# A hybrid HGRN2 and differential attention block: score copies ahead of the q and k update, a forget-gate half one slot later, two remainders three slots later

## The reference

```python
mod = jax.nn.silu(c) @ w_ada[l] + b_ada[l]
shift, scale, gate = jnp.split(mod, 3, axis=-1)
h = rms_norm(x, g_pre[l]) * (1.0 + scale[:, None, :]) + shift[:, None, :]
proj = h @ w_in[l]                       # 1024 x 6144
hq, hf, hi, hg, dq, dk, dv, dg, ma, mb = jnp.split(proj, split_idx, axis=-1)
...
o_a = hgrn2_chunked(hq, k_in, hi, log_f)     # S_t = diag(f_t) S_{t-1} + k_t v_t^T, o_t = S_t^T q_t, 4 heads of 128
o_b = diff_attention(dq, dk, dv, lam)        # (softmax(q1 k1) - lam softmax(q2 k2)) v, causal, 4 heads
...
y = jax.nn.sigmoid(ma) * (o_a @ w_branch_a[l]) + jax.nn.sigmoid(mb) * (o_b @ w_branch_b[l])
x = x + gate[:, None, :] * rms_norm(y @ w_out[l], g_post[l])
```

## Time and profile before

| what | us |
|---|---|
| three runs | 887.14, 888.22, 893.91 (median 888.22) |
| the profiled execution | 888.69 |
| its span, first to last instruction | 886.8 |
| busy: PE, DVE, POOL, ACT | 843.5, 608.5, 478.4, 471.7 |

### The profile page before, as it was taken

How to read it: one execution, slowest core, us unless ns; L and a number is a source line. 1 busy time by engine, 2 the same in 40 slices (tenths; PEclk the granted TensorE clock), 3 DMA queues, 4 the chain that set the end, 5 groups by cost and what they waited for, 6 DMA issues and landing times. The chain is left out here.

```text
span 886.8 us, 13086 instructions
## 1 busy us (share of the span) xinstructions
PE 843.5 (95%) x4781; PEld 664.3 (75%) x4781; DVE 608.5 (69%) x712; ACT 471.7 (53%) x861; POOL 478.4 (54%) x363
## 2 busy tenths in 40 slices
PE   2899889999999999999999999999999999999997
PEld 2687678777777777777777777777788888887885
DVE  3888984788794888694897866864500166697775
ACT  7676323786443875445865336745455641333453
POOL 6054685455464455554545653566787822236884
PEclk9899899999999999999999999999999999999999
DMA  9914131102101101110120121021211561302222
GB/s 327 342 45 147 50 94 48 49 1 72 49 15 58 48 14 59 49 48 24 48 72 1 49 72 32 17 72 49 71 48 48 180 224 47 95 24 95 96 95 95
DMA packets 75586, 68.11 MB, mean 77 GB/s; under 512 B 3652, under 2 KB 65156, under 8 KB 75524
## 3 DMA queue, kind: packets, MB, share of 16 engines
q1 hardware_dynamic: 75408, 67.25, 23.6%
q10 hardware_dynamic: 116, 0.03, 0.0%
HBM read 58.88 MB, written 8.39 MB: 76 GB/s over the span
## 5 line engine op out<-in xcount | busy, mean ns | idle before, releaser
L624 POOL TENSOR_TENSOR w_lo<-w_raw,w_hi 128x512 fp32r<-128x512 f32 x140 | 193.5, 1384 | 258.7 <-ACT w_hi L1197 257.2
L935 PE MATMUL pj<-b_hi,w_hi 128*128 128x512 f32 x712 | 299.7, 421 | 6.3 <-DVE dk L1599 3.4
L937 PE MATMUL pj<-b_hi,w_lo 128*128 128x512 f32 x712 | 279.6, 393 | 0.0
L936 PE MATMUL pj<-b_lo,w_hi 128*128 128x512 f32 x712 | 279.0, 392 | 0.0
L935 PEld LDWEIGHTS pj<-b_hi,w_hi 128*128 128x128 f32 x712 | 134.4, 189 | 49.3 <-issue 12.5
L937 PEld LDWEIGHTS pj<-b_hi,w_lo 128*128 128x128 f32 x712 | 134.2, 188 | 30.0
L936 PEld LDWEIGHTS pj<-b_lo,w_hi 128*128 128x128 f32 x712 | 134.8, 189 | 25.6 <-issue 3.1
L1197 ACT ACTIVATE w_hi<-w_raw 128x512 fp32r<-128x512 f32 x132 | 82.8, 627 | 63.5 <-PE pj L937 57.4
L605 POOL TENSOR_TENSOR w_raw<-w_raw,w_raw 128x512 f32<-128x512 f32 x66 | 91.2, 1382 | 2.9
L685 POOL TENSOR_TENSOR wb_lo<-wb_raw,wb_hi 128x512 fp32r<-128x512 f32 x16 | 22.7, 1422 | 63.3 <-ACT wb_hi L1267 63.3
L1212 ACT ACTIVATE p<-sp,cols 128x1024 f32<-128x1024 f32 (+7 forms) x64 | 46.9, 738 | 0.8
(11 more groups left out here) (290 smaller groups left out, 1647.3 us busy)
## 6 DMA issues: line engine op xcount, KB each, us to landing
w_raw<-in_w_in SPq DMA_DIRECT2D x96, 256.0 KB, 4.1
x_in<-in_x SPq DMA_DIRECT2D x8, 512.0 KB, 7.2
ada<-in_w_ada SPq DMA_DIRECT2D x16, 256.0 KB, 7.1
ada<-in_w_ada SPq DMA_DIRECT2D x8, 512.0 KB, 8.0
ada_g<-in_w_ada SPq DMA_DIRECT2D x8, 512.0 KB, 3.9
res<-in_x SPq DMA_DIRECT2D x8, 512.0 KB, 4.4
out_x<-rows_o SPq DMA_DIRECT2D x7, 512.0 KB, 2.9
o_kepta<-oa SPq DMA_DIRECT2D x4, 512.0 KB, 6.0
```

The lines of the kernel that those rows point to most:

```text
L624: pool.tensor_tensor(w_lo[slot(v)][:, :], raw[:, :], w_hi[slot(v)][:, :].bitcast(F32), ALU.subtract).then_inc(s_wlo, 1)
L935: pe.matmul(bank[:, :], wh, part(bh, kk), start=(fresh and kk == 0), stop=False, skip_group_check=True)
L936: pe.matmul(bank[:, :], wh, part(bl, kk), start=False, stop=False, skip_group_check=True)
L937: last = pe.matmul(bank[:, :], wl, part(bh, kk), start=False, stop=(kk == 3), skip_group_check=True)
```

## The change

Three things are changed.

1. In DVE's part of `lev`, levels 1 to 7: the update of q and k with its wait for `s_upd` comes behind the copy of the scores out of `by`. Both were issued before in the order update, copy, decay pairs; now it is copy, update, decay pairs. It applies to seven levels in each of the rounds 0 to 3.
2. The tables of the forget gates and of the attention's silu gate: half 1 of `F_AT` and `GATEB_AT` goes from slot 13 to slot 14, `MULB_AT` from 14 to 15. Since 14 is the first slot of the loop in which round 0 would be asked for it, `forget` is called for heads 1 to 3 only; head 0's was and is done ahead of the loop.
3. `SUM_LOW_AT`: the remainder of M7 goes from slot 26 to 29, that of M4 from 30 to 33.

No instruction is added or removed on any engine. PE's order and SP's stay the same, POOL's too.

```diff
--- before.py
+++ after.py
@@ -112,15 +112,15 @@
 DVT_AT = (0, 3)
 SSB_AT = (34, 50)
 CLIPB_AT, SQB_AT, OVERB_AT, ROOTB_AT, FINB_AT = (30, 45), (31, 46), (42, 51), (45, 53), (46, 54)
-GATEB_AT, MULB_AT = (10, 13), (11, 14)
-F_AT = (10, 13)
+GATEB_AT, MULB_AT = (10, 14), (11, 15)
+F_AT = (10, 14)
 LEV_AT = [18, 23, 28, 32, 37, 41, 45, 48]
 VT_AT, KT_AT, ST_AT, O_AT, SSA_AT = (21, 26), (50, 51), (53, 54), (56, 57), (61, 63)
 CLIPA_AT, SQA_AT, OVERA_AT, ROOTA_AT, FINA_AT = (58, 59), (59, 60), (63, 70), (73, 73), (75, 76)
 GATEA_AT, MULA_AT = (25, 28), (26, 29)
 GATEA_0, MULA_0 = (30, 33), (31, 34)
 SUM_HIGH_AT = {16: M6, 20: M5, 24: M7, 28: M4}
-SUM_LOW_AT = {17: M6, 21: M5, 26: M7, 30: M4}
+SUM_LOW_AT = {17: M6, 21: M5, 29: M7, 33: M4}
 EVICT_AT = {19: (2, 0), 23: (2, 1), 27: (3, 0), 29: (3, 1)}
 SECOND = [2, 3, 4, 7, 0, 1, 5, 6]
 PIECES = [(0, 2), (2, 4), (4, 8)]
@@ -1304,7 +1304,8 @@
                         act.wait_ge(s_pja, act_reads(at_product(h, 3, M4)))
                         gate_sig(gate_b, 0)
                 for h, e in recurrence(m, F_AT):
-                    forget(h, e)
+                    if h:
+                        forget(h, e)
                 g, x = divmod(n, PROD)
                 if z == 1 and x == 0 and g > 4 * (HEADS + 1):
                     for p, j, half in ((M2, 0, 0), (M7, 1, 1), (M3, 0, 1)):
@@ -1643,8 +1644,6 @@
                         dve.tensor_tensor(q[:, :], q[:, :], f[:, :], ALU.mult).then_inc(s_upd, 1)
                     else:
                         g = LEVELS[n - 1]
-                        dve.wait_ge(s_upd, 8 * h + n)
-                        update(g)
                         dve.wait_ge(s_yd, y_dve(u))
                         if g == 1 and h:
                             dve.wait_ge(s_oah, 2 * h)
@@ -1659,6 +1658,8 @@
                                 src = by[zp, 0:NT * 32].rearrange("p (c b j) -> p c b j", c=NT, j=g)
                                 ins = dve.copy_predicated(dst, mask.to_broadcast([64, NT, 32 // g, g]), src)
                         ins.then_inc(s_yd, 1)
+                        dve.wait_ge(s_upd, 8 * h + n)
+                        update(g)
                         pairs = fs[g].rearrange("p (b s) -> p b s", s=2)
                         then(dve.tensor_tensor(fs[2 * g], pairs[:, :, 0], pairs[:, :, 1], ALU.mult))
                 elif name == "st":
```

## The result

| kernel | median us | runs |
|---|---|---|
| before | 890.92 | 4, 887.14 to 893.91 |
| changed | 903.47 | 4, 902.80 to 903.89 |

The ratio is 1.0147 with a 95% interval of 1.0118 to 1.0177: slower by 1.2 to 1.8%, some 13 us. Forecast were 896.3 and a range up to 902.0. The profiled execution of the changed kernel took 903.89 us around a span of 902.0, 15.2 more than the span before.

The account below looks back on a forecast made before the run. The prediction took PE, busy 95% of the span, as the bound, with DVE setting its waits in round 0. 0 + 7.8 - 3.6 + 0.5 + 3.4 = +8.1 on 888.7, less 0.5 for the median, gave 896.3 us; range 887.0 to 902.0.

Parts of the forecast that it names:

- rounds 1 to 3, exponentials late: ACT's gate block, moved behind the copy of `at`, delays the exponentials and so L751 in slot 17: +2.6 us a round.
- lower clock, whole kernel: PE's clock falls behind two of four new idle pieces, in rounds 0 to 3, at 1.7 us each: +3.4, bounds 0 and 9.
- rounds 1 to 3, copies ahead: Bank `by` copied before the update, so the value products of slots 30 and 43 wait less: -1.2 us a round.
- round 4: Gate b's sigmoid, formerly in the shadow of w_sum, now stands ahead of exponentials that bound PE: +0.5 us.
- the rival that ACT has the room: ACT between slot 13's copy of `at` and slot 14's exponentials inserts no idle time, only gains remain: -6.1, 882.1 us; chance 0.08.
- The one idle piece of 3 us that I named: Round 0, PE's 3.01 us wait ahead of level 3 before the change, followed by the clock at its lower level.
- the clock holds: Same stalls as the forecast but no slow spell on PE: +4.7, 892.9 us; chance 0.26.
- I take 0 for round 0: Round 0: the wait ahead of level 3 moves to stage and dq, DVE ends unchanged: 0 us, bounds -1.5 and +1.5.
- its +1: Round 0: by the DVE and GpSimd exclusion rule, M4's moved remainder pays one more collision, about +1 us instead of 0.
- was hidden behind DVE anyway: Round 0: the 3.0 us lost to the slow clock were hidden behind DVE, so removing them gains nothing.
- every idle piece costs a slow spell and the moved remainders collide twice: Four slow spells at 1.7 us plus 2.2 for collisions on top of 4.7: +13.7, 901.9 us; chance 0.05.
- round 0 pays in full: Round 0's 3.0 us wait and its slow spell both go, -6.0, clock held elsewhere: -1.3 in all, 886.9 us; chance 0.11.

Follow-up runs that it names:

- the filling: Changed kernel with 12 extra products that nobody reads on PE in slot 17 of rounds 1 to 3, ahead of L751: 897.73 us, ratio to before 1.0090.
- `acc_g` moved: Changed kernel with DVE's eight `acc_g` instructions of round 0 at slots 38, 40, ..., 52 instead of 30, 33, ..., 51: 900.09 us, ratio 1.0113.
- filling of slot 34: Copies ahead and remainders later, gates as before, plus unread products in round 0, 8 in slot 34 and 12 in slot 40: 890.44 us (890.14 without them).
- the block behind the exponentials: Changed kernel with half 1 of the forget gates and gate b one slot later still, slot 15, products in 16: 900.25 us, ratio 1.0118.

## Why the prediction was wrong

By its own steps, the changed kernel's profile beside it, in us:

| step | forecast | measured |
|---|---|---|
| round 0 | 0 (-1.5 to +1.5) | +4.3 |
| rounds 1 to 3, exponentials late | +2.6 each | +3.0 at L751, of which 0.55 gained just ahead: +2.5 |
| lower clock, whole kernel | two of the four new idle pieces at 1.7: +3.4 | all four; in rounds 1 to 3 1.6 each by the filling, +4.8; the fourth is in round 0's figure |
| rounds 1 to 3, copies ahead | -1.2 each | -1.1 each |
| round 4 | +0.5 | +0.3 |

*The mechanism on ACT was right*, down to its figures: idle 1.5 to 2 us ahead of w_hi (1.47, and 0.79 ahead of q), L751 3 us late, the wait for `at` under 0.3. The gates alone make the whole loss in the time, and the rival that ACT has the room fell.

*"I take two of four at 1.7"* was the first wrong step. The one idle piece of 3 us that I named was followed by the lower clock, and I set it aside because a sparse unit stood behind it. All four new pieces (3.1, 3.1, 3.1 and 4.8 us), and the 2.17 us for stage too, were followed by it, with dense products behind them. The filling of slot 17 shows cause and size: 4.8 us in three rounds, where I had 3.4 for the whole kernel. The rival "the clock holds" fell. That it was all four is partly luck: with `acc_g` moved, one of three waits of the same 3.1 us had no lower clock behind it, and the other two cost 1.4 and 2.8 us.

*"I take 0 for round 0"* was the second. Three terms were in it. DVE's order up to the add into dq holds the same instructions, from which I took that it ends at the same time, within 1.5; it ended 1.96 later, outside my bounds (at 116.4 us with the start-up left out, where I had written 114 to 116). By the rows above its `acc_g` and gate product came ahead of the end of POOL's work, and POOL's pause became shorter. I had taken the number of collisions with POOL as unchanged; it hangs on when either engine gets there, and POOL's next start hung on DVE's gate product and PE's product. The rule that I cited from the Trainium skill (page "SBUF — State Buffer", section "Who interferes with whom") had the sign: its +1 was nearer than my 0, and by it alone the sum would have been 9.1. But I had put that collision on the remainder of M4, which took 2.28 us as before, so the place was wrong and the sign in part luck. Then the wait for dq of 4.79 us brought the lower clock, +2.0 (L792 starts 2.86 behind the product instead of 1.59, and takes 1.88 instead of 1.13), and last the wait for dk is 0.3 longer. I had written that the slow clock of before "was hidden behind DVE anyway". Of a clock that is low ahead of DVE's wait that is right, and the filling of slot 34 shows it; but I didn't see that the new one stands behind the wait for dq, where DVE in turn waits for PE's next level (3.05 us, 1.02 before), so that nothing hides it. A stall that is moved behind the point that binds costs its lower clock in full, even if its length is the same.

The time that all this makes is 4.3 + 3 x 2.97 + 0.3 = 13.5, near the rival "every idle piece costs a slow spell and the moved remainders collide twice", +13.7, to which I gave 0.05. Its four slow spells came. Its second half is right in size by luck alone: the moved remainders took no longer than before, and round 0's 2.3 us beside the clock are DVE's other instructions and the wait for dk. The rival "round 0 pays in full" fell with the new waits of 2.17 and 4.79 us, which I had forecast at 2.4 and some 4. The medians are 12.6 apart. The parts don't add up plainly in the time: the gates alone lost 13.8 by the medians (12.4 by the profiles, start-up left out), and copies and remainders together nothing, though round 0 was 5.6 us longer in their profile, against 3.3 gained by the copies. What stays open is how much of round 0's part is the change's in an average run: all three profiles of before have the short round 0, and its own runs spread over 887 to 894 us.

## What to carry to other kernels

A block on an engine that stands in the shadow of another engine's result is free only there: find what it fills before moving it, and count what it delays behind the shadow at its full length, less what the unit ahead gains. Where PE is otherwise dense, price an idle piece of 2 to 3 us at its length and at lower clock behind it, here 1.4 to 2 us in most cases, 0 and 2.8 in single ones, unless PE waits again soon after for something that doesn't depend on it. A new order on the engine that binds also changes what it runs beside: the same list of instructions needn't take the same time. And an edit that pays in three rounds and costs in the first is to be made by round, not for all.

## What the runs showed of the hardware

- Idle pieces of PE of 2 to 5 us were mostly followed by the lower clock, with dense products behind them too, but not always. Of nine waits of L751 of 3.1 us (the changed kernel, the gates alone, `acc_g` later) eight were, of three waits of level 0 of 2.13 to 2.15 us (the block behind the exponentials) two. The waits for dk of 1.5 to 1.8 us and pieces of 0.4 to 0.6 us (the silu gate alone, slot 17 filled) were followed by none.
- The same wait of 3.1 us cost 2.8, 1.4 and 0 us of lower clock in three rounds of one execution (`acc_g` later).
- An engine made to do work that nobody reads made the kernel 5.7 us faster.
- In one kernel the fall came later than the wait: with the copies alone level 3 waited 2.79 us and L792 ran at full pace (1.12 us), and the window from 97 to 105 us has a mean of 0.79 all the same.
- Beside POOL a small DVE instruction loses as much as a large one: the decay pairs of 128x64 went from 0.28 to 1.28 us, the `acc_g` of 128x1024 from 1.27 to 2.32, both with a POOL instruction of 1.5 and 1.7 us running at their start. The decay pairs ended 0.1 us behind it.
- A kernel with word for word the same round 0 had it 71.4 us long in five profiles and 76.3 in one.
